# Logits of two heads or two maps in the two row halves of TensorE, in a two-layer trunk with differential, banded and chunked attention

## What is computed

```
s = einsum(q, k) * ATTN_SCALE + bias                # A: 4 heads, two maps each, head size 64
p = softmax(where(allowed, s, -inf))                # allowed: key chunk (64 tokens) <= query chunk
attn = p[map 0] - lam * p[map 1];  o = attn @ v     # v is 128 wide; then a norm, a gate
...
p = softmax(concat(s, sink))[..., :WINDOW]          # B: 8 heads on 2 key heads, 2 chunks of 64 keys
...
s = einsum(q, k) * ATTN_SCALE + bias                # C: 16 heads, 9 chunks of 64 keys
p = softmax(where(start + koff >= 0, s, -inf));  o = p @ v
...
x = x + (o * silu(gate)) @ w_out                    # after each layer
```

## Time and profile before

| what | us |
|---|---|
| median of 3 runs | 2793.43 |
| lowest, highest | 2789.69, 2796.32 |
| the profiled execution | 2793.07 |
| its span in the profile | 2791.4 |
| p0, A, B, o0 | 0 to 631, to 1031, to 1158, to 1367 |
| p1, C, o1 | 1367 to 2117, to 2581, to 2791 |

### The profile page before, as it was taken

The page is one execution under the profiler, slowest core; times in us unless marked ns, Lnnn a source line. Parts: engine busy times, 40 slices in busy tenths (PEclk is TensorE's granted clock), DMA queues, the critical chain, the costliest instruction groups (busy, mean ns, idle before and its releaser), DMA issues. The chain is left out here.

```text
span 2791.4 us, 43476 instructions
## 1 busy us (share of the span) xinstructions
PE 2604.9 (93%) x16328; PEld 2250.3 (81%) x16328; DVE 1197.6 (43%) x2561; ACT 868.3 (31%) x1971; POOL 327.1 (12%) x228
## 2 busy tenths in 40 slices
PE   5999999996999888799899999999996999999898
PEld 4788888995887777588688888889996888888787
DVE  6411111105788767555421111111012777777565
ACT  4211111005777766412221111111002555555121
POOL 1121212100000003111111121211100001101000
PEclk9999999998999999799899999999997999999899
DMA  5444523119345508566453433222226768775552
GB/s 175 122 133 129 173 68 96 52 47 208 80 83 117 118 26 218 156 239 219 152 167 113 128 121 113 87 64 79 59 44 135 173 158 182 167 178 116 174 211 76
DMA packets 237856, 359.65 MB, mean 129 GB/s; under 512 B 59524, under 2 KB 136112, under 8 KB 236896
## 3 DMA queue, kind: packets, MB, share of 16 engines
q1 hardware_dynamic: 223808, 311.43, 40.5%
q0 software_dynamic: 11168, 41.95, 5.3%
q10 hardware_dynamic: 2688, 3.67, 0.6%
HBM read 223.75 MB, written 138.70 MB: 130 GB/s over the span
## 5 line engine op out<-in xcount | busy, mean ns | idle before, releaser
L524 PE MATMUL p_acc<-p_h_hi,p_w_hi 128*128 128x512 f32 x1440 | 565.0, 392 | 16.4 <-DVE p_h_lo L468 16.4
L524 PE MATMUL p_acc<-p_h_hi,p_w_lo 128*128 128x512 f32 x1440 | 561.6, 390 | 0.0
L524 PE MATMUL p_acc<-p_h_lo,p_w_hi 128*128 128x512 f32 x1440 | 561.6, 390 | 0.0
L524 PEld LDWEIGHTS p_acc<-p_h_hi,p_w_hi 128*128 128x128 f32 x1440 | 271.5, 189 | 74.8 <-DVE p_h_lo L468 19.7
L524 PEld LDWEIGHTS p_acc<-p_h_hi,p_w_lo 128*128 128x128 f32 x1440 | 271.0, 188 | 56.6
L524 PEld LDWEIGHTS p_acc<-p_h_lo,p_w_hi 128*128 128x128 f32 x1440 | 271.4, 188 | 55.5
L238 DVE SCALAR_TENSOR_TENSOR p_lo_out<-p_acc,p_hi_out 128x512 fp32r<-128x512 f32 x116 | 80.1, 691 | 486.1 <-ACT p_hi_out L222 486.1
L1244 ACT ACTIVATE c_prob<-c_logits,c_neg_max 128x640 f32<-128x640 f32 (+4 forms) x256 | 185.4, 728 | 207.1 <-DVE c_neg_max L1219 207.0
L1219 DVE CUSTOM_DVE_ANT_0 c_logits<-c_logits,c_bias 128x640 f32<-128x640 f32 (+4 forms) x256 | 185.8, 762 | 122.4 <-PE c_logits L1140 122.2
L222 ACT ACTIVATE p_hi_out<-p_acc 128x512 fp32r<-128x512 f32 x116 | 69.5, 599 | 510.3 <-PE p_acc L524 495.1
L521 PE MATMUL p_acc<-p_w_hi,p_h_lo 128*128 128x256 f32 (+1 forms) x768 | 225.4, 293 | 3.1 <-issue 3.1
(11 more groups left out here) (167 smaller groups left out, 4004.6 us busy)
## 6 DMA issues: line engine op xcount, KB each, us to landing
scr_qh<-p_hi_out SPq DMA_DIRECT2D x116, 256.0 KB, 2.5
scr_ql<-p_lo_out SPq DMA_DIRECT2D x116, 256.0 KB, 2.9
scr_gt<-p_f_out SPq DMA_DIRECT2D x128, 128.0 KB, 1.9
ready_w<-in_w_in_odd POOLq DMA_DIRECT2D x16, 1024.0 KB, 6.7
c_k<-scr_qh SPq DMA_DIRECT2D x60, 256.0 KB, 8.3
c_k<-scr_ql SPq DMA_DIRECT2D x60, 256.0 KB, 9.9
p_w_raw<-in_w_in_even POOLq DMA_DIRECT2D x10, 1024.0 KB, 6.8
o_x<-in_x SPq DMA_DIRECT2D x16, 512.0 KB, 4.3
```

The lines of the kernel that those rows point to most:

```text
L524: last = nc.tensor.matmul(acc[v % 4][:, :], wt[:, half, c * n + cc * P:c * n + (cc + 1) * P], ht[:, c, b * BLK:(b + 1) * BLK], **flags)
```

## The change

- Logits: a tile of high rows and a tile of low rows each hold two heads (in A the two maps of a head) in their two row halves. Three products are made (high by high, high by low, low by high), each for both heads in turn: six matmuls over 64 rows in place of four over 128. The fourth product, low by low, is left out.
- A: `parts[g]` numbers parts in twos, one of each map. `qk(g, 0)` now makes the far part of both maps, `qk(g, 1)` the near part of both (nothing up to 8 key tiles), and both stand where they stood. VectorE takes both far maxima, the near maximum of map 0, the difference of step g-1, and the near maximum of map 1. An exponential waits for its near maximum, as before. A block is loaded with 5 DMAs of 128 rows. `share` has 8 slots for 7, `own` 5 for 7.
- B and C: a step is one tile of a pair of heads, the logits of one head each in `logits[0]` and `logits[1]`; `qk(s)` waits for both maxima of step s-1 (`max_done`, 2s). The maximum writes to `prob` in SBUF, and the exponential works there. `MAIN` is 3: VectorE copies three transposed tiles of each half, ScalarE two. Outputs go out in one DMA of 128 rows every four steps; q, k, values and bias are loaded for a pair of heads; GpSimd's weight loads of C wait for the first loads. `post.load` comes behind the first store of the last pair of heads, into buffers of `share`.
- Output stage: products go to the buffers `gated` and `mix`, no longer in place; its operands lie in `share`.

```diff
@@ diff_attn @@
-        own = st.sb("own", [P, 7, SEQ], F32R)
...
+        own = st.sb("own", [P, 5, SEQ], F32R)
+        q_sb = [[of[:, x, :] for x in range(2)] for of in (share, own)]
+        k_sb = [[of[:, 2 + x, :] for x in range(2)] for of in (share, own)]
...
-        def load_map(eng, h, m, n):
...
+        def load_part(eng, h, n, x):
             cols = slice(n * BLK, (n + 1) * BLK)
...
+            b, loaded, part_ = h % 2, head_loaded[h % 2][n], scr[("qh", "ql")[x]]
+            eng.dma_start(q_sb[b][x][:, cols].bitcast(F32), part_[h * P:(h + 1) * P, cols]).then_inc(loaded, 16)
+            eng.dma_start(k_sb[b][x][:, cols].bitcast(F32), part_[A_W + h * P:A_W + (h + 1) * P, cols]).then_inc(loaded, 16)
...
-            def qk(g, m):
+            def qk(g, which):
...
+                n, at, tiles = parts[g][which]
+                if n + 1 >= RING:
+                    pe.wait_ge(moved, n + 1 - RING + 1)
+                for first in range(0, tiles, TPB):
...
+                    for turn, (x, y) in enumerate(((0, 0), (0, 1), (1, 0))):
+                        for m in range(2):
+                            rows = slice(m * HD, (m + 1) * HD)
+                            last = nc.tensor.matmul(logits[(n + m) % RING][:, first * P:(first + some) * P], q_sb[h % 2][x][rows, i * P:(i + 1) * P],
+                                                    k_sb[h % 2][y][rows, keys], start=turn == 0, stop=turn == 2)
+                last.then_inc(qk_done, 1)
...
             for g in range(G + 3):
+                if g < G and len(parts[g]) > 1:
+                    maximum(g, 0, 0)
+                    maximum(g, 0, 1)
                 if g < G:
-                    maxima(g, 0)
+                    maximum(g, len(parts[g]) - 1, 0)
                 if 1 <= g <= G:
                     difference(g - 1)
                 if g < G:
-                    maxima(g, 1)
+                    maximum(g, len(parts[g]) - 1, 1)
                 if g >= 3:
                     output(g - 3)
@@ band_attn @@
-        shifted = st.sb("shifted", [P, 2, WIDE + SPARE]) if sinks else None
+        MAIN = 3
+        FAR = max(0, back + 1 - MAIN)
...
+            for hp in range(HP):
+                for r in range(STORES):
+                    store(hp, r)
...
+                    if r == 0 and hp == HP - 1:
+                        sp.wait_ge(stored[0], 16 * (STORES // 2 * hp + 1))
+                        sp.wait_ge(stored[1], 16 * (STORES // 2 * hp))
+                        sp.wait_ge(qk_done, TILES * hp)
+                        post.load(sp)
...
+                pool.wait_ge(first_loaded[-1], 16 * (LOADS + 1))
...
-                if k >= 2:
-
-                    pe.wait_ge(max_done if sinks else exp_done, k - 1)
-                s_ps = logits[k % 2]
+                if s >= 1:
+                    pe.wait_ge(max_done, 2 * s)
...
-                    for s in range(2):
-                        last = nc.tensor.matmul(s_ps[:, lo:hi], q_sb[b][:, i * P:(i + 1) * P],
-                                                k_sb[b][s][:, tile * P:tile * P + hi - lo], start=s == 0, stop=s == 1)
+                    for n, (x, y) in enumerate(((0, 0), (0, 1), (1, 0))):
+                        for half in range(2):
+                            rows = slice(half * HD, (half + 1) * HD)
+                            last = nc.tensor.matmul(logits[half][:, lo:hi], q_sb[b][x][rows, i * P:(i + 1) * P],
+                                                    k_sb[kb][y][rows, tile * P:tile * P + hi - lo], start=n == 0, stop=n == 2)
...
+                nc.vector.tensor_tensor_reduce(out=prob[:, j, 0:n + SPARE], in0=logits[half][:, END - n:END + SPARE], in1=bias[:, b, WIDE - n:WIDE + SPARE],
+                                               scale=1.0, scalar=HIGHEST, op0=ALU.add, op1=ALU.min, accum_out=neg_max[:, j:j + 1]).then_inc(max_done, 1)
...
+                nc.scalar.activation(p, p, ACT.Exp, bias=neg_max[:, j:j + 1], scale=-1.0,
+                                     accum_out=sums[:, 2 * hp + half, i:i + 1]).then_inc(exp_done, 1)
@@ output @@
+        gated, mix = st.sb("gated", [P, KC, P]), st.sb("mix", [P, KC, P])
...
+                nc.vector.tensor_tensor(mix[:, :, :], o_sb[b % 2][:, :, tokens], gated[:, :, :], ALU.mult).then_inc(mixed, 1)
...
+                share = both.enter_context(nc.sbuf_tensor("share0", [P, 8, SEQ], F32R))
```

More of the change, by code:

```diff
@@ L582, in diff_attn @@
         for g, (h, i) in enumerate(steps):
[L583 to L589, removed]
+            n = i + 1
+            last = min(n, PART // P)
+            parts[g] = []
+            for at, tiles in [(0, n - last)] * (n > last) + [(n - last, last)]:
+                parts[g].append((part, at, tiles))
+                part += 2
         turns, diffs = {}, {}
@@ L655, in _ @@
         def _(pe):
-            def qk(g, m):
+            def qk(g, which):
                 h, i = steps[g]
-                if m == 0 and i % TPB == 0:
+                if which >= len(parts[g]):
+                    return
+                if which == 0 and i % TPB == 0:
                     pe.wait_ge(head_loaded[h % 2][i // TPB], 16 * LOADS * (h // 2 + 1))
[L661 to L665, removed]
-                        for s in range(2):
[L667 to L670, removed]
+                n, at, tiles = parts[g][which]
+                if n + 1 >= RING:
+                    pe.wait_ge(moved, n + 1 - RING + 1)
+                for first in range(0, tiles, TPB):
+                    some = min(TPB, tiles - first)
+                    keys = slice((at + first) * P, (at + first + some) * P)
+                    for turn, (x, y) in enumerate(((0, 0), (0, 1), (1, 0))):
[4 more added lines that the diff above has]
+                last.then_inc(qk_done, 1)
             left = [0, 0]
@@ new lines, in maximum @@
+                if which == 0 and m == 1 and g >= 2:
+                    dve.wait_ge(diff_done, diffs[g - 2][-1][0] + 1)
+                dve.wait_ge(qk_done, n // 2 + 1)
+                to = prob[m][g % (3 - m)][:, at * P:(at + tiles) * P]
+                source = logits[(n + m) % RING][:, 0:tiles * P]
+                if which < len(parts[g]) - 1:
+                    nc.vector.tensor_tensor_reduce(out=to, in0=source, in1=zeros[:, 0:tiles * P], scale=1.0, scalar=HIGHEST,
+                                                   op0=ALU.add, op1=ALU.min, accum_out=part_max[:, j:j + 1]).then_inc(moved, 1)
+                    return
@@ L889, with __init__ @@
 class OutputReady:
[L892 removed]
+    def __init__(self, nc, ctx, name, scr, heads, share):
         def sb(what, shape):
```

393 lines of the change are left out of this document (167 added, 226 removed).

## The result

The changed kernel takes 2876.32 us (median of 4 runs, 2873.0 to 2880.4) against 2791.62 for the kernel before in the same comparison: ratio 1.0302, 95% interval 1.0282 to 1.0321, slower by 84.7 us. The forecast was 2857 (+64), range 2800 to 2915. The profiled executions, with which the sum was made, stand at 2873.0 and 2793.1: +79.9.

The account below looks back on a forecast made before the run. It took 16-head band_attn as TensorE-bound and diff_attn as bound by chains through three engines. Terms of +102 - 5 (diff_attn), +5 - 10 - 7 (small-head band_attn), -8 - 8 - 5 (16-head) made +64: 2793.1 to 2857 us, range 2800 to 2915.

Parts of the forecast that it names:

- A's cycle: diff_attn, two-part steps: a loop between near parts through both maxima, difference, exponential, copies and TensorE; 10.4 us mean a step.
- A is +102, ends +81 and +125 (some clock loss): diff_attn: two-part steps +106 us over four heads, shorter steps -4; upper end if TensorE's idling loses clock.
- the cycle doesn't close: Rival for diff_attn: unseen slack keeps it at 93 us a head, total 2751 us; chance 0.10.
- loads in turn: Rival for paired logits: the two row halves' weight loads go one after the other, +77 us, total 2934; chance 0.06.
- no overlap: Rival for paired logits: row halves do not run side by side at all, total about 3020 us; chance 0.04.
- C: band_attn on the 16 heads: -8 us from its steps and -8 from its start.
- Its start: Start of band_attn on 16 heads: fewer tiles of rows and later weight loads shorten DMA waits, -8 us.
- the change of shape: Switching TensorE's tiling, once more per band_attn step and two to four times per diff_attn step: 0.19 us each.
- the steps of one to four tiles: band_attn on 16 heads, narrow steps: one or two tiles save 0.11 us, pay 0.19; 16 give 1 us back.
- B: band_attn on the small heads: +5 us from its steps, -10 from fewer loads and stalls of stores.
- The ends: Ends of both band_attn stages: loads moved from ahead of the last store, -7 us (small heads) and -5 (16 heads).
- The start of A: Start of diff_attn: 13 DMAs for block 0 become 5, where TensorE waited 19.24 us; -5 us.

Follow-up runs that it names:

- the new order: Changed kernel with diff_attn's steps reordered on TensorE, VectorE and ScalarE (near part before second transposes, difference before near maxima, copies before exponentials): 2751.2 us, ratio 0.9844.
- e_warm12: Changed kernel plus twelve matmuls nobody reads at the end of each two-part step of diff_attn: 2859.7 us, ratio 1.0237 to the kernel before.
- e_load_late: Changed kernel with post.load of both band stages moved back ahead of the stage's last store: 2875.7 us.
- e_change: Changed kernel plus one small matmul ahead of each band-stage step's logits, over full rows in every second pair of heads, rows 0 to 63 otherwise: 2930.9 us.

## Why the prediction held, and where it was off

**A's cycle** is shown: each edit to its links moved A the way that the walk gave. The sizes a head, with the walk's in brackets: near part earlier -24 us (-18), later +5 to +9 (+5), difference out of it -7 (-7.5), the new order -31 (-22). The near part first and the new order gain more than the walk says, and the granted clock of A rises with them, to 0.96 and 0.95 from 0.85. The term was mis-sized, +137 for +102. The step that was short is "A is +102, ends +81 and +125 (some clock loss)": the paces were taken at full clock. With dummy matmuls that keep the clock at 0.98, seven of eight steps fall on the forecast's 9.3 to 11.1 us; they take 71 to 73 us of a head where the changed kernel takes 78 to 79, 27 us less over the four heads. Without them the clock is 0.83 there, and the two-part steps take 34.0 us a head more than before where 26.6 were forecast: 30 us over four heads, of the 35 that the term was short. So some 27 of them go with the clock. (e_warm12 brought 17 in the net, since the last step of a head and the first of the next are longer in it.) The rival that the cycle doesn't close is refuted, and so are those of loads in turn and of no overlap.

The total of the two profiled executions, +80 for +64 (the medians have +85), came nearer than A's own term, and that is in part luck: A was 35 us over its term, while B and C together gave 12 more than forecast and p1 gave 7 that no term had.

**C** gained 24.7 us for 16. Its start came about as forecast, and in another place: the first matmul stands 11.7 to 11.8 us behind p1 in both, and what got shorter are the two waits behind it, 7.6 and 5.8 us before (both for loads) and 3.5 (for a maximum) and 2.5 (for a load) after, -7.4 for -8. The first two rows are of before, the last two of the changed kernel:

```profile
2135.37 2.08 PE L1140 MATMUL c_logits<-c_k,c_q 128*128 128x128 f32 x8 [7.62 <-DMA c_v<-scr_v]
...
2148.33 2.08 PE L1140 MATMUL c_logits<-c_k,c_q 128*128 128x384 f32 x6 [5.77 <-DMA c_v<-scr_v]
```

```profile
2240.36 1.01 PE L1121 MATMUL c_logits<-share 64*128 64x256 f32 x6 [3.48 <-DVE c_neg_max L1194]
...
2244.45 1.65 PE L1121 MATMUL c_logits<-share 64*128 64x128 f32 x12 [2.46 <-DMA c_v<-scr_v]
```

If each step is held against the median at its place in a head, all that lies over the medians fell from 17.8 to 8.0 us, these waits with it. The steps themselves, by their medians, gave 15 us for 8.5: the change of shape cost 0.16 and not 0.19 (0.289 - 0.16 = 0.13 a full step, 0.14 measured), and the steps of one to four tiles gained 1 us where I had them lose 1. **B**: by its medians +2.1 for +5, over them 14.3 to 3.9, -10.3 for -10. **The ends**: -7.1 for -7 and -3.8 for -5. e_load_late shows 6.3 and 2.8 of these to be the place of the loads; that the rest is the single store is not shown. **The start of A**: 19.2 to 13.9, and 13.8 to 14.8 in the twelve profiles of the experiments, which all have the new loads.

**p1** is no term of the forecast and yet gave 7.0 us. The profile of before has a stall there (first two rows), the changed kernel none; but of the twelve experiments, whose p1 is the same code, one (e_change, last two rows) has it too, at the same point of p1:

```profile
2016.47 0.38 PE L521 MATMUL p_acc<-p_w_hi,p_h_hi 128*128 128x256 f32 x1 [1.44 <-DVE p_f_out L244]
...
2019.91 0.58 PE L521 MATMUL p_acc<-p_w_hi,p_h_lo 128*128 128x256 f32 x1 [3.06 <-issue]
```

```profile
2161.84 0.38 PE L521 MATMUL p_acc<-p_w_hi,p_h_hi 128*128 128x256 f32 x1 [1.93 <-issue]
...
2165.16 0.58 PE L521 MATMUL p_acc<-p_w_lo,p_h_hi 128*128 128x256 f32 x1 [2.47 <-issue]
```

p1 took 740.2 and 739.8 us in these two, and 732.2 to 733.2 in the other twelve profiles. So the stall comes and goes with the execution in code that is the same, and need not be the change's: without it the profiled difference would be +87, and the medians have +85. How often it comes in the kernel before, one profile can't tell.

## What to carry to other kernels

When a split of work is regrouped (here from "both parts of map 0, then of map 1" to "far parts, then near parts"), each place in a hand-written order that was right for the old groups has to be looked at again: one group that was fine in mid-step for the second map closed a loop through three engines once both maps hung on it.
